# Taps on rows and banded matrices from memory in a two-layer attention and convolution kernel

## The reference, cut to what matters

```python
def conformer_conv_branch(h, w_in, w_dw, b_dw, g_ln, b_ln, w_o):
    a, bgl, g = jnp.split(h @ w_in, 3, axis=-1)
    u = a * jax.nn.sigmoid(bgl)
    u = lax.conv_general_dilated(u, w_dw, window_strides=(1,), padding=[(CONV_PAD, CONV_PAD)],
                                 dimension_numbers=('NWC', 'WIO', 'NWC'),
                                 feature_group_count=CONV_W) + b_dw
    u = jax.nn.silu(layer_norm(u, g_ln, b_ln)) * jax.nn.silu(g)
    return u @ w_o
```

## Time and profile before

| | us |
|---|---|
| median of 3 runs | 2989.02 (2988.29 to 2990.73) |
| profiled execution, own time | 2987.92 |
| its span | 2986.1 |
| TensorE busy | 2877.6 |
| VectorE busy | 1997.5 |
| ScalarE busy | 1434.5 |
| GpSimd busy | 385.2 |
| `conv_in`, first matmul | 2146.59 |
| `conv_in`, first matmul of `conv_out` | 2783.91 |

### The profile page before, as it was taken

How to read it: one execution, slowest core, us unless ns; L and a number is a source line. 1 busy time by engine, 2 the same in 40 slices (tenths; PEclk the granted TensorE clock), 3 DMA queues, 4 the chain that set the end, 5 groups by cost and what they waited for, 6 DMA issues and landing times. The chain is left out here.

```text
span 2986.1 us, 42933 instructions
## 1 busy us (share of the span) xinstructions
PE 2877.6 (96%) x14429; PEld 2395.0 (80%) x14429; DVE 1997.5 (67%) x3275; ACT 1434.5 (48%) x3029; POOL 385.2 (13%) x467
## 2 busy tenths in 40 slices
PE   6999999999999999999999999999899989899898
PEld 4888888788888888888888888778787878788687
DVE  6664654567767776766767677644438797986875
ACT  5554646455565556655555565634511111122553
POOL 0000000022212221222122212200001011012000
PEclk9999999999999999999999999999999999999899
DMA  7657564620212112111211111145522322223563
GB/s 269 208 197 265 176 211 170 218 57 29 68 43 76 33 49 59 59 49 33 76 43 51 46 43 57 50 166 172 204 81 66 91 77 78 82 70 111 178 201 122
DMA packets 225832, 323.66 MB, mean 108 GB/s; under 512 B 81584, under 2 KB 143296, under 8 KB 224320
## 3 DMA queue, kind: packets, MB, share of 16 engines
q1 hardware_dynamic: 220992, 312.35, 32.4%
q10 hardware_dynamic: 4608, 8.39, 0.7%
HBM read 223.03 MB, written 97.66 MB: 107 GB/s over the span
## 5 line engine op out<-in xcount | busy, mean ns | idle before, releaser
L1313 DVE TENSOR_TENSOR at_ptlo<-at_T,at_pthi 128x512 fp32r<-128x512 f32 x576 | 396.9, 690 | 303.9 <-ACT at_pthi L1191 300.4
L1175 ACT ACTIVATE at_prob<-at_S,at_nmax 128x512 f32<-128x512 f32 x634 | 407.5, 659 | 341.3 <-DVE at_nmax L1289 341.3
L1191 ACT ACTIVATE at_pthi<-at_T 128x512 fp32r<-128x512 f32 x576 | 349.0, 608 | 210.7 <-PE at_T L1057 210.7
L1278 DVE TENSOR_REDUCE at_mx<-at_S 128x1 f32<-128x512 f32 x634 | 390.7, 631 | 73.3 <-PE at_S L1030 62.5
L1057 PE MATMUL at_T<-ident,at_prob 128*128 128x128 f32 x2304 | 346.0, 272 | 4.2 <-DVE at_ptlo L1313 4.2
L1057 PEld LDWEIGHTS at_T<-ident,at_prob 128*128 128x128 f32 x2304 | 279.3, 140 | 69.4 <-DVE at_ptlo L1313 13.4
L186 PE MATMUL ci_ps<-h1hi,ci_whi 128*128 128x512 f32 x768 | 301.2, 392 | 5.3 <-DVE h1lo L2108 5.3
L187 PE MATMUL ci_ps<-h1lo,ci_whi 128*128 128x512 f32 x768 | 300.5, 391 | 0.0
L188 PE MATMUL ci_ps<-h1hi,ci_wlo 128*128 128x512 f32 x768 | 300.0, 391 | 0.0
L186 PE MATMUL at_O<-at_pthi,at_vhi 128*128 128x512 f32 x576 | 270.0, 469 | 0.6 <-DVE at_og L1327 0.5
L677 DVE TENSOR_TENSOR fr_wlo<-fr_w,fr_whi 128x1024 fp32r<-128x1024 f32 (+1 forms) x99 | 115.1, 1167 | 218.3 <-ACT fr_whi L533 218.0
(11 more groups left out here) (292 smaller groups left out, 6084.8 us busy)
## 6 DMA issues: line engine op xcount, KB each, us to landing
fr_w<-in_w_front SPq DMA_DIRECT2D x75, 512.0 KB, 4.3
at_wmod<-in_w_mod SPq DMA_DIRECT2D x32, 512.0 KB, 3.5
cv_w<-in_cv_w_in SPq DMA_DIRECT2D x24, 512.0 KB, 4.3
fr_w<-in_w_front SPq DMA_DIRECT2D x24, 384.0 KB, 4.1
values<-fr_ob SPq DMA_DIRECT2D x36, 256.0 KB, 3.0
at_vst<-values SPq DMA_DIRECT2D x8, 1152.0 KB, 7.2
fr_w_mod<-in_w_modr SPq DMA_DIRECT2D x17, 512.0 KB, 5.3
fr_x<-in_x SPq DMA_DIRECT2D x16, 512.0 KB, 6.9
```

The lines of the kernel that those rows point to most:

```text
L1175: nc.scalar.activation(prob[:, j % 2, i, k], bank(h, j, i, c)[:, 0:k.stop - k.start], ACT.Exp, scale=SCALE, bias=nmax[:, i % 2:i % 2 + 1], ...
L1191: nc.scalar.activation(dst, T[:, (n + SLOTS * j) % 2], ACT.Copy).then_inc(s_hi, 1)
L1278: nc.vector.tensor_reduce(mx[:, i % 2, c:c + 1], bank(h, j, i, c)[:, 0:k.stop - k.start], AXX, ALU.max).then_inc(s_mx, 1)
L1313: nc.vector.tensor_tensor(ptlo[:, kt % 3], T[:, (n + SLOTS * j) % 2], pthi[:, kt % 3].bitcast(F32), ALU.subtract).then_inc(s_lo, 1)
```

## The change

Four things are changed together. (1) The banded matrices come whole from memory (`bands`, 128x640 for each chunk), one load per chunk into `band`, which has three buffers and shares its bytes with `blo`; ScalarE rounds it to `bhi`, VectorE subtracts in place. The mask, the small taps tensor, its split and all work of GpSimd go. (2) The tapped groups keep `u` as plain rows (`u_rows`), so that a tap is one instruction on 2048 contiguous elements; at the end ScalarE turns `acc` into phases, 8 copies of 256 elements with a stride of 8 (`turn`), each stored by itself, in groups 2, 4 and 6 after gates 2 and 3. (3) The preparation of the next group's first chunk is moved: ScalarE's `u_high` stands after gate 1, VectorE's `band_and_low` after gate 2. (4) `TAP_STEPS` is new: 18 taps in groups 1, 3, 5 and 13 in groups 2, 4, 6, where they end at gate 0; the sums of a tapped group run two steps later in groups 3 and 5.

```diff
-TAP_STEPS = [(g, s, n) for a in (1, 3, 5) for g, row in ((a, (0, 1, 1, 1, 1, 1, 1, 2, 2, 2, 2, 2)), (
-    a + 1, (1, 1, 1, 1, 1, 1, 1, 1, 2, 2, 2, 1))) for s, n in enumerate(row)]
+TURNED_IN = (2, 4, 6)
+TAP_STEPS = [(g + a, s, n) for g in (0, 2, 4) for a, row in (
+    (1, (1, 2, 1, 2, 1, 2, 1, 2, 2, 1, 2, 1)), (2, (2, 1, 2, 1, 2, 1, 2, 1, 1))) for s, n in enumerate(row)]
...
-        taps = sb("taps", [P, CH, OFFS * PHASES])
-        thi, tlo = sb("thi", [P, CH, OFFS * PHASES], F32R), sb("tlo", [P, CH, OFFS * PHASES])
-        bhi, blo = (sb(n, [P, 2, OFFS, CCH, PHASES], F32R) for n in ("bhi", "blo"))
+        bhi = sb("bhi", [P, 2, OFFS * P], F32R)
+        band = placed(nc, "ci_band", [P, 3, OFFS * P], F32, 0)
+        blo = sb("blo", [P, 3, OFFS * P], F32R)
...
+            def load_band(g, q):
+                n = nth(g, q)
+                if n >= 3:
+                    sp.wait_ge(s_cv, n - 2)
+                sp.dma_start(band[:, n % 3], net.bands[g * CH + q]).then_inc(s_band[n % 3], 16)
...
-            def store_acc(i):
-                sp.wait_ge(s_tap, (i + 1) * CONV_K)
-                sp.dma_start(net.z_phases[TAPPED[i]], acc[:]).then_inc(s_acc, 16)
+            def store_turned(i, phase):
+                n = i * PHASES + phase
+                sp.wait_ge(s_turn, n + 1)
+                sp.dma_start(net.z_phases[TAPPED[i], :, phase], zr[:, n % 2]).then_inc(s_acc[n % 2], 16)
...
                 for n in range(CH):
+                    if i is not None and (not last or n + 1 < CH):
+                        reload_z(i, n + 1 if last else n)
                     if c is not None:
+                        if n + 2 < CH:
+                            load_band(c, n + 2)
                         reload_u(c, n)
...
                     for x in TAIL:
                         if isinstance(x, int):
+                            if x + 2 < CH:
+                                load_band(g, x + 2)
                             reload_u(g, x)
...
                 nc.scalar.activation(uhi[:, q % 2, HALO:HALO + NCOL], raw[:, q % 4], ACT.Copy).then_inc(s_uhi, 1)
+                act.wait_ge(s_band[n % 3], 16 * (n // 3 + 1))
+                nc.scalar.activation(bhi[:, q % 2], band[:, n % 3], ACT.Copy).then_inc(s_bhi, 1)
...
+            def turn(i, phase):
+
+                n = i * PHASES + phase
+                act.wait_ge(s_tap, (i + 1) * CONV_K)
+                if n >= 2:
+                    act.wait_ge(s_acc[n % 2], 16 * (n // 2))
+                if i and phase < 2:
+                    act.wait_ge(s_d, at[TAPPED[i - 1], CH - 2 + phase] + 1)
+                nc.scalar.activation(zr[:, n % 2], acc[:].rearrange("p (n s) -> p s n", s=PHASES)[:, phase],
+                                     ACT.Copy).then_inc(s_turn, 1)
...
                     for b in range(NBLK):
                         gate(g, b)
+                        if i is not None and b < lag(g):
+                            square_before(TAPPED[i], CH - lag(g) + b)
+                        for x in turned_at(g, b):
+                            turn(*x)
+                        if b == 1 and g in BY_PE:
+                            u_high(g, 0)
...
             def band_and_low(g, q):
                 n = nth(g, q)
-                if n >= 2:
-                    dve.wait_ge(s_cv, n - 1)
-                nc.vector.tensor_tensor(bhi[:, q % 2], *banded(thi[:, q].bitcast(F32)), ALU.mult).then_inc(s_bhi, 1)
                 dve.wait_ge(s_uhi, n + 1)
                 nc.vector.tensor_tensor(ulo[:, q % 2, HALO:HALO + NCOL], raw[:, q % 4],
                                         uhi[:, q % 2, HALO:HALO + NCOL].bitcast(F32), ALU.subtract).then_inc(s_ulo, 1)
+                dve.wait_ge(s_bhi, n + 1)
+                nc.vector.tensor_tensor(blo[:, n % 3], band[:, n % 3], bhi[:, q % 2].bitcast(F32),
+                                        ALU.subtract).then_inc(s_blo, 1)
...
-                if c is not None:
-                    band_and_low(c, 0)
...
                         run_taps(g, CH + b)
+                        if b == 2 and g in BY_PE:
+                            band_and_low(g, 0)
...
-        @block.gpsimd
-        def _(pool):
-            pool.wait_ge(s_const, CONST)
-            for p in range(len(BY_PE)):
-                pool.wait_ge(s_tlo, p + 1)
-                for q in range(CH):
-                    n = p * CH + q
-                    if n >= 2:
-                        pool.wait_ge(s_cv, n - 1)
-                    nc.gpsimd.tensor_tensor(blo[:, q % 2], *banded(tlo[:, q]), ALU.mult).then_inc(s_blo, 1)
```

More of the change, by code:

```diff
@@ L1700, in conv_in @@
         s_ust, s_gst, s_zst = net.sems("ci_u_stored", 2), net.sems("ci_g_stored", 2), net.sems("ci_z_stored", 2)
[L1701 to L1705, removed]
+        s_band = net.sems("ci_band_in", 3)
+        s_raw, s_zr, s_acc = net.sems("ci_raw_in", 4), net.sems("ci_z_in", 2), net.sems("ci_acc_stored", 2)
+        (s_const, s_pad, s_whi, s_wlo, s_ab, s_g, s_sig, s_mul, s_uhi, s_ulo, s_bhi, s_blo, s_cv,
+         s_z, s_zero, s_z0, s_d, s_zs, s_dsq, s_qs, s_ut, s_tap, s_turn) = (net.sem("ci_" + n) for n in (
+             "const", "pad", "whi", "wlo", "ab", "g", "sig", "mul", "uhi", "ulo", "bhi", "blo",
+             "cv", "z", "zero", "z0", "d", "zs", "dsq", "qs", "ut_in", "tap", "turned"))
         s_h = net.sems("ci_h_in", 2 * (NBLK - 1))
@@ L1745, in nth, with turned_at @@
             return BY_PE.index(g) * CH + q
[L1747 to L1757, removed]
+        taps_at = {(g, s): n for g, s, n in TAP_STEPS}
+        def turned_at(g, b):
+            if g not in TURNED_IN or b not in (2, 3):
+                return ()
+            return [(TURNED_IN.index(g), x) for x in range((b - 2) * PHASES // 2, (b - 1) * PHASES // 2)]
         first_tap = {}
@@ L1838, in reload_z @@
                 if q == 0:
-                    sp.wait_ge(s_acc, 16 * (i + 1))
-                if n >= 2:
+                    for k in range(2):
+                        sp.wait_ge(s_acc[k], 16 * (i + 1) * PHASES // 2)
+                if n >= 2 and q >= 2:
                     sp.wait_ge(s_d, at[TAPPED[(n - 2) // CH], (n - 2) % CH] + 1)
                 sp.dma_start(zr[:, n % 2], net.z_chunks[TAPPED[i] * CH + q]).then_inc(s_zr[n % 2], 16)
[L1844 to L1850, removed]
             for g in range(GROUPS):
                 c, i, last = banded_group(g), summed_group(g), g == GROUPS - 1
[L1854 to L1860, removed]
+                if i is not None and last:
                     reload_z(i, 0)
                 for n in range(CH):
[L1863 to L1866, removed]
+                    if i is not None and (not last or n + 1 < CH):
+                        reload_z(i, n + 1 if last else n)
                     if c is not None:
+                        if n + 2 < CH:
+                            load_band(c, n + 2)
                         reload_u(c, n)
@@ L1985, in _ @@
                         w_high(g, G)
-                    if i is not None:
-                        square_before(TAPPED[i], n)
+                    if i is not None and n >= lag(g):
+                        square_before(TAPPED[i], n - lag(g))
                 if c is not None:
@@ L2052, in tap @@
                     if i:
-                        dve.wait_ge(s_acc, 16 * i)
+                        dve.wait_ge(s_turn, PHASES * i)
+                    nc.vector.tensor_scalar(acc[:], u, tw[:, g, 0:1], tb[:, g:g + 1], ALU.mult, ALU.add).then_inc(s_tap, 1)
                 else:
                     dve.wait_ge(s_tap, n)
-                for a, b, d_s, d_n in pieces:
-                    z, u = acc[:, a:b], ut[:, a + d_s:b + d_s, d_n:d_n + NCOL]
-                    if t == 0:
-                        last = nc.vector.tensor_scalar(z, u, tw[:, g, 0:1], tb[:, g:g + 1], ALU.mult, ALU.add)
-                    else:
-                        last = nc.vector.scalar_tensor_tensor(out=z, in0=u, scalar=tw[:, g, t:t + 1], in1=z, op0=ALU.mult,
-                                                              op1=ALU.add)
-                last.then_inc(s_tap, 1)
+                    nc.vector.scalar_tensor_tensor(out=acc[:], in0=u, scalar=tw[:, g, t:t + 1], in1=acc[:], op0=ALU.mult,
+                                                   op1=ALU.add).then_inc(s_tap, 1)
             def run_taps(g, s):
@@ L2142, in _ @@
                         w_low(g, G)
-                    if i is not None:
-                        tapped_sums(i, n)
+                    if i is not None and n >= lag(g):
+                        tapped_sums(i, n - lag(g))
                     run_taps(g, n)
@@ L2159, in _ @@
                         gate(g, b)
+                        if i is not None and b < lag(g):
+                            tapped_sums(i, CH - lag(g) + b)
                         run_taps(g, CH + b)
+                        if b == 2 and g in BY_PE:
+                            band_and_low(g, 0)
                 else:
@@ L2750, in layout @@
```

(5 more changed lines are left out.)

78 lines of the change are left out of this document (37 added, 41 removed).

## The result

The changed kernel takes 2967.78 us (median of 6 runs, 2964.50 to 2970.15) against 2988.47 us for the kernel before, run beside it (6 runs). The ratio is 0.9931, 95% interval 0.9918 to 0.9943: some 21 us faster. The profiled execution took 2967.01 us, with a span of 2965.2.

What follows compares the result with a forecast made beforehand. TensorE, busy 96%, was taken as the bound, pausing for VectorE's late order at group starts. Profiled 2987.92 - 32.2 + 0.5 + 8.2 = 2964.4; the same -23.5 from the median 2989.02 gives 2965.5, stated as 2965; range 2956 to 2977.

Steps and rivals of the forecast that it cites:

- First chunk during the gates: Starts of groups 2, 4, 6, 7: all 32.24 us of TensorE's losses go; 0.5 us charged for groups 4 and 6.
- VectorE's walk for group 3: VectorE's work summed through group 3, the tightest: low band ready at T+70.6, wanted by TensorE at T+70.72; just fits.
- rival 3: VectorE late in groups 3 and 5: a tap costs 2.7 us, not 2.26; +18 us, 2983; chance 0.09.
- Taps on rows, GpSimd: VectorE's taps in one piece and no GpSimd beside them: a pair 4.63 us for 6.43; no charge beyond the walk.
- Bands whole: Whole bands loaded from memory: no bandwidth problem; ScalarE copies of 0.71 us each, hidden except in the tail.
- rival 4: Every band late inside the groups, 24 chunks waiting once landings pass 11.6 us; about 2999 at 13; chance 0.06.
- Turning: ScalarE's `acc` copies and stores in groups 2, 4, 6: group end runs 5 us over, first tap to about T+5.7, hidden.
- Tail: Group 7's last convolutions: bands queued behind gate stores delay convolutions 2 and 5, 7.0 us, plus 1.2 clock: +8.2.
- rival 1: Tail's loads land late in queues filled by `w_o` loads: both pauses grow by 2.9 us; 2973; chance 0.13.

Runs made afterwards that it cites:

- experiment 5: The kernel before with only the next group's first chunk prepared during the gates; old taps, masks, GpSimd and tail stay: 2966.63 us, ratio 0.9925.
- experiment 4: The changed kernel with the preparation of a group's first chunk back at the beginning of that group: 2984.47 us, ratio 0.9983.
- experiment 6: The changed kernel with each tap but the first split into eight instructions of 256 elements: 3007.70 us, ratio 1.0065.
- experiment 8: The changed kernel with GpSimd kept busy by 40 products on a tile of its own that nobody waits for: 2969.82 us, ratio 0.9938.
- Experiment 7: The changed kernel with the eight `w_o` weight loads issued only behind convolutions 5, 6 and 7 of the tail: 2970.71 us, ratio 0.9940.
- experiment 2: The changed kernel with bands loaded one chunk earlier in group 7's tail, three ahead of the gates: 2959.47 us, ratio 0.9898.
- experiment 3: On top of experiment 2, the tail's chunks prepared three ahead in three buffers of their own: 2962.73 us, ratio 0.9911.
- experiment 9: On top of experiment 2, the `w_o` weight loads issued behind convolutions 2, 3 and 4: 2959.28 us, ratio 0.9897.
- 10: On top of experiment 2, four buffers instead of two for the evicted `z` in the tail: 2959.29 us, ratio 0.9898.

## Why the prediction was right, step by step

*Range and mechanism.* 2965 was predicted, 2967.78 measured, in the range of 2956 to 2977; -23.5 us for the stage, -22.45 in the profile. Three errors of the tail partly cancel in that (below): its landings were charged too long, its second issue too early, the clock too low.

*First chunk during the gates: -32.2 + 0.5.* Right in size. With the tail's change of +9.1 (below) taken from -22.45, the groups give -31.5. Experiment 5 shows that the move carries the gain; experiment 4, that without it two thirds are lost.

*VectorE's walk for group 3.* It had the band subtracted at T+70.6, wanted at T+70.72, T being the group's start. The group started at 2359.40; the timeline of VectorE:

```profile
2412.25 1.08 DVE L2038 TENSOR_TENSOR ci_ub<-ci_ps,ci_sig 128x512 f32<-128x512 f32 x1
...
2424.41 4.72 DVE L2073 SCALAR_TENSOR_TENSOR ci_acc<-ci_ut,ci_tap_w,ci_acc 128x2048 f32<-128x2048 f32 x2
2429.05 0.42 DVE L2111 TENSOR_TENSOR ci_ulo<-ci_raw,ci_uhi 128x256 fp32r<-128x256 f32 x1
2429.39 0.82 DVE L2114 TENSOR_TENSOR ci_blo<-ci_band,ci_bhi 128x640 fp32r<-128x640 f32 x1
```

Gate 0's product starts at T+52.85 (the walk: 52.7), the band is done at 2430.21, T+70.8. TensorE starts the convolution at 2430.31, 0.19 us late. The 0.5 us charged were enough, and experiment 6 shows what rival 3 would have cost: a tap of 3.25 us loses the whole gain. Rival 3's own sum is loose. It lets the stalls begin at a tap of 2.35 us, but behind step 7's product the walk has seven taps and 0.1 us to spare, which gives 2.28. The kernel stands at that edge.

*Taps on rows, GpSimd.* Right: a tap takes 2344 ns on the mean, and experiment 8 puts the price of GpSimd's work at 3.2 us of the stage.

```profile
L2073 DVE SCALAR_TENSOR_TENSOR ci_acc<-ci_ut,ci_tap_w,ci_acc 128x2048 f32<-128x2048 f32 x90 | 210.9, 2344 | 1.2
```

The prediction put 6.43 us of a pair against 4.63 and named GpSimd alone; 0.3 of the difference were the pieces. It gave no number to what taps and bands add beyond the move; experiment 5 does, 10.5 us in the groups.

*Bands whole.* ScalarE's copy takes 0.72 to 0.74 us (0.71 said), VectorE's subtraction 0.82. Inside the groups the loads land after 3.5 us in the median and 6.1 at most, where rival 4 needed 11.6; ScalarE waits for them 4.0 us in all, TensorE never. Rival 4, every band late, had no part in it.

*Turning.* The waits for the two buffers' stores are there, and cost TensorE nothing. But they were priced too low: ScalarE waits nine times, 22.4 us in all, up to 3.7 for the 2.5 said, a copy takes 0.69 us for 0.4, and the first tap of group 3 starts at T+8.7 where T+5.7 was said:

```profile
2368.11 1.35 DVE L2070 TENSOR_SCALAR ci_acc<-ci_ut,ci_tap_w,ci_tap_b 128x2048 f32<-128x2048 f32 x1 [5.55 <-ACT ci_zr L1953]
```

Step 1 starts at T+10.9, so 3 us of error were hidden, with 0.8 to spare. That they were hidden is partly luck; in experiment 4, without the move, the same error is paid in group 7.

*Tail: +8.2.* It was +9.1: pauses of 4.43 and 5.40 us and 3.7 of half clock, 13.5 against 4.44. Convolution 2 was forecast 8.4 us after 0 and came 8.01 after it, since from the band's issue to ScalarE's copy it took 3.73 us for 4.2; convolution 5 came 8.96 after 3, since gate 2's store kept the queue to 3.4 us after convolution 3, not 2.6. The clock took 3.7 where 3.0 were charged. The 1.8 of half clock in the tail of before are not sure either: experiment 5, with the same pauses, lost 0.2, and against that the tail costs 10.7. Experiment 7 confirms the place in the queue, against rival 1's cause, the weights. Of rival 1 the full queues are real, but they decide only once the bands are early (experiments 2, 3, 9 and 10).

## What to carry to other kernels

When one engine sits at 97%, look for the first use after a boundary of the schedule and prepare it one step before the boundary: that one move, alone, was the whole 22 us here. Price the rest of a change stage by stage: the other parts together won 10 us in the middle, and the bands' loads lost 9 to 11 at the end, where issue and use fell into the same step; one chunk of distance for the loads in an in-order queue gave 7 of them back. And move the load together with its use: preparing earlier without loading earlier only moved ScalarE's wait for the load forward, and was slower.

## What the runs showed of the hardware that had not been expected

The first tap, an operation with one tensor as input, took 1.35 us on 2048 contiguous elements of float32; before, in the phase layout, it took 2132 ns on 1792:

```profile
L2059 DVE TENSOR_SCALAR ci_acc<-ci_ut,ci_tap_w,ci_tap_b 128x1792 f32<-128x1792 f32 x3 | 6.4, 2132 | 0.0
```

The two-input tap took 2344 ns on 2048, and 3.25 us in eight pieces. The Trainium skill ("VectorE: DVE Perf Modes", Mode 2×_2P) has a mode for operations with one tensor input, in which both read ports fetch that one tensor. The 1.35 us, little over half of 2.34, agree with it. No run here shows why the phase layout did not get it.

The length of a pause alone did not decide whether the clock fell behind it. Behind those of 4.27 and 5.25 us idle it fell to 1.2 GHz for most of 4 to 5 us, and behind the two of 0.92 and 0.93 in experiment 9 it stayed at 1.00. In between it went both ways. Behind 2.00 us in experiment 2 it was 0.56 in the convolution that followed, behind 2.06 us in experiment 3 it stayed at 1.00. Behind 1.76 us in the tail of the kernel before it fell, behind 1.75 at the same place in experiment 5 it did not. And the two pauses of 3.17 us in experiment 4, before the first convolutions of groups 4 and 6, are followed by 1.00 and by 0.76:

```profile
2434.50:2441.70 7.20, 7.20 (x39) 6.29 (x40) 7.13 (x8) 1.71 (x4) 0.00 (x0) 1.00 0.82 249
2582.80:2590.00 7.20, 7.20 (x32) 6.44 (x33) 7.13 (x8) 1.71 (x4) 0.00 (x0) 0.76 0.72 201
```

No run here shows what decides it. For pauses of about 1.8 to 3.2 us a forecast has to carry both, nothing and some 1.6 us of half clock.
